# Two decoder layers on eight cores: how the inputs are loaded, how two pairs of steps are ordered, and where the last block ends

## The reference

```
sh1, sc1, g1, sh2, sc2, g2 = ada_modulation(c, w_ada[i], b_ada[i])   # silu(c) @ w_ada + b_ada
h = rms_norm(x) * norm_g * (1 + sc1) + sh1
layer 0:  y = ((mean of the last 2/4/8/16 tokens, by channel group) - h) @ w_pool * pool_scale
layer 1:  u, v = split(gelu(h @ w_in + b));  v = layer_norm(v)
          y = (u * (tril(W_s) @ v per chunk of 128 tokens + b_s)) @ w_out
x = x + g1 * y
h = rms_norm(x) * norm_g * (1 + sc2) + sh2
x = x + g2 * (relu(h @ w1) ** 2) @ w2          # D_FF = 4096
end:      y = rms_norm(x) * final_g
```

## Time and profile before

| | us |
|---|---|
| median of 3 runs | 1456.17 (1374.86, 1456.17, 1598.68) |
| the profiled execution, own time | 1374.97 |
| its span on the slowest core | 1373.4 (the 8 cores: 1369.1 to 1373.4) |
| PE busy | 1267.1 (92%) |
| DVE busy | 750.5 (55%) |
| ACT busy | 628.5 (46%) |
| POOL busy | 44.9 (3%) |

### The profile page before, as it was taken

One profiled execution on the slowest core, in us unless ns is written; L12 is line 12 of the kernel. 1 busy time (PEld: TensorE's weight loads), 2 busy tenths in 40 slices (PEclk: granted clock), 3 DMA queues, 4 the chain that ended last, 5 costly groups with the idle time before them and its releaser, 6 DMA issues.

```text
span 1373.4 us, 21544 instructions; the slowest of 8 cores (1369.1 to 1373.4 us)
## 1 busy us (share of the span) xinstructions
PE 1267.1 (92%) x7518; PEld 669.8 (49%) x7518; DVE 750.5 (55%) x1406; ACT 628.5 (46%) x1142; POOL 44.9 (3%) x87
## 2 busy tenths in 40 slices
PE   0289999999999999998998897999999999999994
PEld 0045665555555555554343443555545555554552
DVE  0288675545445454555466547765545454454566
ACT  0376843333333333488635543733333333333463
POOL 1000100000000000000000000000000000000000
PEclk9989999999999999999999998999999999999997
DMA  9968765425353333503000006403113030200024
GB/s 185 252 135 137 123 109 105 75 49 93 60 94 55 69 67 57 93 1 62 1 1 1 8 17 115 95 14 62 32 31 62 1 63 16 47 1 0 1 108 153
DMA packets 22791, 91.06 MB, mean 66 GB/s; under 512 B 2704, under 2 KB 9104, under 8 KB 14608
## 3 DMA queue, kind: packets, MB, share of 16 engines
q0 software_dynamic: 9392, 67.34, 28.4%
q1 hardware_dynamic: 13296, 22.35, 5.4%
HBM read 145.43 MB, written 11.01 MB: 114 GB/s over the span
## 4 chain that ended last, share of the span: by engine, by line
PE 87%; ACT 4%; DVE 3%; DMA 3%; issue 2%; another core or an unknown queue 1%; DVEq 0%; POOL 0%; ACTq 0%; SPq 0%; POOLq 0%
PE ps L930 34%; PE ps L956 34%; PE ps L1180 4%; PE ps L1095 4%; PE ps L775 3%; DMA xT_sb<-x_pack 3%; PE ps L606 2%; PE ps L1066 2%; ACT hT_sb L635 1%; PE ps L568 1%; DVE hT_sb L625 1%; DVE xT_sb L1210 1%; PE ps L1097 1%; ACT arena L1071 0%
## 5 line engine op out<-in xcount | busy, mean ns | idle before, releaser
L672 DVE SCALAR_TENSOR_TENSOR xT_sb<-ps,modT,xT_sb 128x384 f32<-128x384 f32 (+2 forms) x720 | 459.2, 644 | 450.6 <-PE ps L956 405.5
L956 PE MATMUL ps<-arena,ring 128*128 128x384 bf16 (+1 forms) x2592 | 520.2, 345 | 0.0
L930 PE MATMUL ps<-hT_sb,ring 128*128 128x384 bf16 (+2 forms) x2592 | 520.0, 345 | 0.0
L936 ACT ACTIVATE arena<-ps 128x384 bf16<-128x384 f32 (+2 forms) x324 | 170.4, 528 | 499.2 <-PE ps L930 498.7
L956 PEld LDWEIGHTS ps<-arena,ring 128*128 128x128 bf16 x2592 | 252.1, 98 | 216.9
L930 PEld LDWEIGHTS ps<-hT_sb,ring 128*128 128x128 bf16 x2592 | 251.3, 98 | 216.2
L938 ACT ACTIVATE arena<-arena 128x384 bf16<-128x384 bf16 (+3 forms) x324 | 181.2, 562 | 26.4
L603 ACT ACTIVATE sq<-xT_sb 128x384 bf16<-128x384 f32 (+3 forms) x208 | 105.3, 545 | 127.3 <-DVE xT_sb L672 62.1
L625 DVE TENSOR_TENSOR hT_sb<-xT_sb,rstd 128x768 bf16<-128x768 f32 (+2 forms) x80 | 75.8, 1007 | 94.0 <-ACT rstd L617 94.0
L606 PE MATMUL ps<-sq,ones 128*128 128x384 bf16 (+3 forms) x208 | 54.4, 381 | 52.6 <-ACT sq L603 50.4
L1095 PE MATMUL ps<-ring,hT_sb 128*128 128x512 bf16 x272 | 69.1, 400 | 11.6 <-ACT arena L1071 9.3
(11 more groups left out here) (88 smaller groups left out, 447.3 us busy)
## 6 DMA issues: line engine op xcount, KB each, us to landing
ring<-w_pack POOLq DMA_DIRECT2D x62, 1024.0 KB, 9.5
xT_sb<-x_pack SPq DMA_DIRECT2D x3, 1536.0 KB, 36.4
y_pack<-xT_sb SPq DMA_DIRECT2D x12, 384.0 KB, 2.5
xT_sb<-x_pack SPq DMA_DIRECT2D x2, 2048.0 KB, 59.7
y_pack<-xT_sb SPq DMA_DIRECT2D x8, 512.0 KB, 2.9
ring<-w_pool POOLq DMA_DIRECT2D x1, 1024.0 KB, 24.4
arena<-sp_pack POOLq DMA_DIRECT2D x1, 736.0 KB, 18.3
arena<-w_pool POOLq DMA_DIRECT2D x1, 512.0 KB, 14.3
```

What stands on the lines that cost most here:

```text
L672: nodes.append(S.op("dve", lambda e: e.scalar_tensor_tensor(out=xs, in0=P_(v)[:, 0:n], scalar=mcol(l, vG, dco), in1=xs, op0=ALU.mult, op1= ...
L930: mms = [(lambda e, dc=dc: e.matmul(P_(v)[:, 0:n], pv(key, 512)[:, dc, fc * 128:(fc + 1) * 128], hT.ap()[:, dc, c0:c0 + n], start=(dc == 0 ...
L936: ev = S.op("act", lambda e: e.activation(out=av, in_=P_(v)[:, 0:n], func=AF.Relu), reads=[(v.key, 0, 1)], writes=ak, cost=c_act(n), vbs=[v])
L956: mms.append((lambda e, fc=fc, av=av: e.matmul(P_(v)[:, 0:w], pv(key, 1024)[:, fc, dco * 128:(dco + 1) * 128], av, start=(fc == 0), stop=( ...
```

## The change

1. x of groups 0 to 2 is issued first, and x of groups 3 and 4 later in SP's list. The first weight piece (w0) gets a wait for x of group 2, and w5 (ada 8) one for x of group 4. On SP no wait stands before x of groups 3 and 4.
2. The Exp of an inverse root follows its Ln at once in ACT's list (`glue`), and the planner puts an operation that needs another function table 2.5 us back.
3. The affine of groups 3 and 4 of the first MLP norm, and of the norm before the SGU for all groups, goes from ACT to DVE: 56 operations.
4. `mix_part` of the group before is woven with the `v_tile`s.
5. In the MLP of layer 1 the first `mm1` output goes to another arena slot, and the scratch `BX` of `v_out` is moved; both free space so that the MLP may start earlier. The last block takes the groups in the order 4, 1, 2, 0, 3, and group 3 ends as 256 and then 128 columns. The multiplies of `final` get a priority 30 us later.
6. All costs and latencies of the planner are given new values, and some start times, so all lists change.

```diff
-LAT = {"pe": 0.12, "act": 0.22, "dve": 0.17, "pool": 0.2, "sp": 0.2}
+LAT = {"pe": 0.16, "act": 0.28, "dve": 0.24, "pool": 0.3, "sp": 0.3}
+TABLE_BIAS = 2.5
...
+                for n in (avail[e] if forced[e] is None else [forced[e]]):
...
+                        if e == "act" and n.table is not None and n.table != cur_table:
+                            p += TABLE_BIAS
...
+            forced[e] = n.glue
...
-    return 0.17 + n * 0.00102          # c_act
+    return 0.07 + n * 0.00085
...
+    for g in range(3):
+        load_x(g)
...
+    GATE = {("ada", 0, 2): 2, ("ada", 0, 8): 4}
...
+        if key in GATE:
+            t0, n = GR[GATE[key]]
+            gate = XK(t0, t0 + n)
...
-                     writes=[(v.key, 0, 1)], stream="w%d" % i, cost=0.85, vbs=[v], nbytes=1 << 21,
+                     reads=gate, writes=[(v.key, 0, 1)], stream="w%d" % i, cost=0.53, vbs=[v], nbytes=1 << 21,
...
-        S.op("act", lambda e: e.activation(out=R, in_=R, func=AF.Exp, scale=-0.5), reads=RK, writes=RK, cost=c_act(n), table="ln")
+        ev.glue = S.op("act", lambda e: e.activation(out=R, in_=R, func=AF.Exp, scale=-0.5), reads=RK, writes=RK, cost=c_act(n), table="ln")
...
-    load_upto(("wpool", 0, 0))
+    load_upto(("ada", 0, 5))
+    S.base = -5.0
+    load_x(3, after=[prev[0]])
+    load_x(4, after=[prev[0]])
...
-        affine(0, 1, hb(g), n)
+        affine(0, 1, hb(g), n, "act" if g < 3 else "dve")
...
+        if l == 1:
+            asl[0] = 2
+        steps = [(b, g) for b in range(8) for g in ((4, 1, 2, 0, 3) if l == 1 and b == 7 else range(5))]
...
+                if l == 1 and b == 7 and g == 3:
+                    for (lo, w, sp) in ((0, 256, False), (256, 128, True)):
+                        for f in mm2(l, b, t0 + lo, w, 0, 0, ao, n, lo):
+                            f()
+                        after(g, lo, w, sp)
+                    return
...
-            affine(l, k, hb(g), n)
+            affine(l, k, hb(g), n, "dve" if k == 0 else "act")
...
-        GX, BX = 6144, 14336
+        GX, BX = 6144, BINV
...
+                weave(vts, mix_part(g - 1))
                 out_part(g - 1)
                 norm(1, 1, g - 1)
...
+            S.base = S.clk + 30.0
             for dc in (d, d + 1):
```

More of the change, by code:

```diff
@@ L64 @@
     __slots__ = ("eng", "subs", "deps", "cost", "prio", "stream", "vbs", "idx", "table", "after", "nbytes", "evac",
-                 "start", "fin", "done", "left", "users", "pos", "snap", "sig", "sigval", "swaits")
+                 "start", "fin", "done", "left", "users", "pos", "snap", "sig", "sigval", "swaits", "glue")
     def __init__(self, eng, cost, prio, stream, idx):
@@ L79, in __init__ @@
         self.evac = []
+        self.glue = None
         self.done = False
@@ L187, in schedule @@
         cur_table = None
+        forced = {e: None for e in ENGS}
         order = []
@@ L595, in build_program, with stats @@
     rsi = [0]
-    def stats(t0, n, extra_dst=None):
+    def stats(t0, n, own=False):
         v = S.vb("ps")
@@ L982, in mlp @@
         pend = []
-        steps = [(b, g) for b in range(8) for g in range(5)]
+        if l == 1:
+            asl[0] = 2
+        steps = [(b, g) for b in range(8) for g in ((4, 1, 2, 0, 3) if l == 1 and b == 7 else range(5))]
+        prevg = None
         for (b, g) in steps:
@@ L1005, in mlp @@
                 weave(m1, pend)
-                if b == 7 and g > 0 and after is not None:
-                    after(g - 1)
+                if b == 7 and prevg is not None and after is not None:
+                    after(prevg)
+                prevg = g if b == 7 else None
                 pend = m2
+                if l == 1 and b == 7 and g == 3:
[4 more added lines that the diff above has]
+                    return
             if hooks is not None:
@@ L1040, in sgu_setup @@
              stream="s_bsp", cost=0.1, nbytes=524288)
-        S.op("pool", lambda e: e.dma_start(out=binv[0:1, :], in_=d_binv.ap()), writes=[AR(BINV, BINV + 2048)], stream="s_binv", cost=0.85, nbytes=4096)
+        S.op("pool", lambda e: e.dma_start(out=binv[0:1, :], in_=d_binv.ap()), writes=[AR(BINV, BINV + 2048)], stream="s_binv", cost=0.53, nbytes=4096)
         for gi in range(4):
@@ L1140, in mix_part, with one @@
         npr = n if g < 4 else 256
-        for cc in range(8):
+        def one(cc):
             gi = cc // 2
@@ L1167, in mix_part @@
             S.evac(ch, ev)
+        return [lambda cc=cc: one(cc) for cc in range(8)]
     def out_part(g):
@@ L1202, in sgu, with final @@
         norm(1, 1, 4)
-    def final(g):
+    def final(g, off=0, nn=None, own=False):
         t0, n = GR[g]
-        R, RK = stats(t0, n)
+        t0 += off
+        if nn is not None:
+            n = nn
+        R, RK = stats(t0, n, own)
         for d in range(0, NDC, 2):
+            S.base = S.clk + 30.0
             for dc in (d, d + 1):
```

97 lines of the change are left out of this document (50 added, 47 removed).

## The result

The changed kernel takes **1322.41 us** (median of 4 runs, 1321.95 to 1323.73; the profiled execution 1323.73, its span 1322.2). Beside it the kernel before took 1374.86, 1375.70, 1456.17 and 1598.68 us; the last two are executions in which the cores of a die run at a lower clock, so the comparison uses the first two: **ratio 0.9617, 95% interval 0.9594 to 0.964**, about 53 us less. In a second comparison it was 0.9612 (0.9598 to 0.9627).

A forecast was written before the change was run, and what follows sets the result against it. PE was taken as the bound except for idle time at the start (63.5 us), in the SGU (24.2) and after the last mm1 chain (18.6). 1375 - 24 - 16 - 6 = 1329 us, range 1308 to 1359.

The forecast's parts named there:

- I predict at the level of the lowest: Whole kernel: the forecast starts from 1375 us, the lowest of three runs shown, not from their median of 1456.
- Start, -24: Loading before steady PE work: x of groups 0 to 2 alone lands at 20, PE starts at 53.5; 24 us gained.
- "DVE has less" slack: Start, 53.5 to 106 us: DVE's new list holds about 50 us of work; 3.5 us taken off the gain.
- SGU, -16: SGU: of 32 us lost to PE waits and half clock, 16 remain; 16 us gained, bounds 4 and 24.
- 2 x 2.3 + 3 + 2 idle, 2 for things I cannot see, 4 of clock: SGU loss left: two norms at 2.3 us, norm before the SGU 3, group 4's mixing 2, unseen 2, half clock 4.
- End, -6: After the last mm1 chain: DVE's work without idle time plus the last output, 23.4 us against 29.7; 6 us gained.
- Weights as the start's bound: Start: x of group 4 lands near 77, w5 at 87; start gives 14, total 1339 us; chance 0.12.
- SGU given back: SGU: weave and affines make DVE wait for POOL's root, mixing queued behind; SGU gives 4, total 1341 us; chance 0.12.
- DVE as the bound: Whole kernel: uncovered affines cost DVE 40 us and v tiles 29; total 1414 us, slower; chance 0.03.
- order not held: Start: x DMAs from SP alone run at 190 GB/s, gaining no rate; start -14, at worst 1350 us; chance 0.08.
- Descriptors: POOL's DMA issue: runs of moved affines on DVE delay pieces 3 us each, at most 10 reaching PE; 1339 us; chance 0.03.
- the sum with the drain, 1324: SGU norms: a 1.38 us drain per table load, 2.66 in all, three norms each losing 5.3 us; total 1324 us.

## Why the prediction was right and wrong

**Which step failed.** The sum came to 1329, a gain of 46 on 1375; measured were 1322, a gain of 53, or 51.2 in the spans. The mechanisms came as forecast, and the term of the sum that was mis-sized is the SGU's: -16 forecast, -24.7 measured, because the 16 us of loss that I left in it were about 9. The start was 3 us too large and the end nearly right, so the error of the sum is smaller than that of its largest part, and that is luck.

**The level.** The other step that doesn't hold is the one behind the sum, "I predict at the level of the lowest". It gives a time, but the only summary of the kernel before that stands beside it is the median of 1456, and it names no gain. Against 1456 the forecast of 1329 reads as 8.7% less, and what the change brings is 3.8%. The gain should have been written out as 46 of 1375, 3.3%; the 81 us between 1456 and 1375 have nothing to do with the change.

**Start, -24, measured -20.8.** The mechanism held: pool matmuls after w3, w3 33 us after w0's issue (I had 33.5), no wait on a piece later, w5's gate harmless. What was mis-sized is the landing of x of group 2: 24.9 instead of 20. I had 5.77 MB at 338 GB/s throughout. In windows of 1.5 us from the start the queues moved

```profile
GB/s 0 112 176 177 283 284 313 284 344 313 367 330 333 351 412 212 106 265 316 291 247 129 148 187 149 195 146 189 200 194 276 359 244 229 175 158 200 158 206 181
```

so it was about half the rate until 6 us, and it fell to 212 and 106 from 22.5 us on, before the last x was there. The copy of `sp_tail`, issued at 6.7 us, ran beside from there on. Everything behind moved by these 5 us: the pool matmuls came at 59.3 instead of 53.5, and the first `mm1` at 116.0, where I had 104 to 112. "DVE has less" slack was right: it was busy 29.6 of 30 us from 80 to 110, yet PE lost only 0.4 us there. When the pool matmuls were made earlier, PE lost 3 us at 90 to 100.

**SGU, -16, measured -24.7.** Here the sum failed. Table loads went from 20 to 12 as forecast, and no wait for DVE above 2 us is left. But I kept 16 us of loss, "2 x 2.3 + 3 + 2 idle, 2 for things I cannot see, 4 of clock", and 6.5 idle and about 2 of clock were left. The first of these held (2.6 and 2.5 us, two norms). The other terms were about nothing: the norm before the SGU lost no time, and neither would it have with its affines on ACT. I had costed every wait as if its cover stayed what it was. The runs show that covers overlap: with the root kept together the weave was worth nothing more, and the two together 12 us. The wait for the layer norm of group 4 went whole once the two MLP chains stood before it (4 us, by the kernel with the addresses undone). Affines on DVE took 0.41 us for 512 columns (I had 0.4) and cost nothing.

```profile
L656 DVE TENSOR_SCALAR hT_sb<-hT_sb,modT 128x512 bf16<-128x512 bf16 x11 | 3.7, 406 | 0.0
```

**End, -6, measured -5.7,** 24.3 us against my 23.4. The size was right, and the reason only in part: I gave it to the split and the new order. These are worth nothing when the multiplies are put off, and 1.9 us came from the new costs, which the sum didn't price.

**The rivals.** Weights as the start's bound, SGU given back, DVE as the bound, order not held: none came. The last is the closest: x of group 2 did come 5 us late, but at 286 GB/s from 2 to 20 us and not at 190. Descriptors: POOL's DMA issue took 0.537 us at the median and 0.672 at most, 0.527 and 0.662 before. But none of the issues falls into one of the seven runs of moved affines; the nearest ends 0.5 us before one. So this rival had no occasion, and the lock that the Trainium skill describes (SBUF — State Buffer, Who interferes with whom) is neither seen nor tested here. The drain before a table load (the Trainium skill, ScalarE: Activation LUTs, What ACT_TABLE_LOAD costs) isn't in the trace: after a Square ended at 615.6 the load starts at once, and Gelu directly behind it. That the sum with the drain, 1324, lies nearer to the measured time is chance.

```profile
614.26 1.33 ACT L618 ACTIVATE sq<-xT_sb 128x384 bf16<-128x384 f32 x3
615.60 1.28 ACT L1102 ACT_TABLE_LOAD   x1
616.89 0.58 ACT L1102 ACTIVATE arena<-ps,vecs_sb 128x384 bf16<-128x384 f32 x1
```

## What to carry to other kernels

Price edits that cover the same wait together. Root and weave undone alone were worth 4 to 5 and 0 us here and 12 together, so the sum over the single prices was less than half. Where loads compete, the early one isn't safe by being issued first; hold the later ones back until what they would pass has landed, and count bytes read. And say in the forecast against which of the shown times its gain is meant.
